# Stacking the recurrence's gate product in 64-channel blocks, and taking the next turn's first strip ahead, in a one-core fp32 two-block model kernel

## What is computed

```
proj = rmsnorm(x, ln1_g) @ w_in
b_a, c_a, x_a, x_b, g_b, gate_a_logit, gate_b_logit = split(proj)
y_a = b_a * causal_depthwise_conv(c_a * x_a, conv_a_w)          # 3 taps
u_b = causal_depthwise_conv(x_b, conv_b_w, conv_b_b)            # 4 taps and a bias
xh  = u_b as (512, 16 heads, 64)
r   = sigmoid(einsum('bshd,hde->bshe', xh, w_a) + b_a)          # 64 x 64 per head
i   = sigmoid(einsum('bshd,hde->bshe', xh, w_x) + b_x)
a   = exp(-8 * r * softplus(-lam));  b = sqrt(1 - a*a) * (i * u_b)
h_t = a_t * h_{t-1} + b_t                                       # scan over the 512 tokens
y_b = h * gelu(g_b)
```

## Time and profile before

| | |
|---|---|
| median of 3 runs | 1701.06 us |
| the profiled execution's own time | 1705.36 us |
| its span, first to last instruction | 1703.6 us |
| TensorE busy | 1671.0 us (98%) |
| GpSimd busy | 819.4 us (48%) |
| VectorE busy | 880.0 us (52%) |
| ScalarE busy | 643.8 us (38%) |

### The profile page before, as it was taken

One profiled execution on the slowest core, in us unless ns is written; L12 is line 12 of the kernel. 1 busy time (PEld: TensorE's weight loads), 2 busy tenths in 40 slices (PEclk: granted clock), 3 DMA queues, 4 the chain that ended last, 5 costly groups with the idle time before them and its releaser, 6 DMA issues.

```text
span 1703.6 us, 21182 instructions
## 1 busy us (share of the span) xinstructions
PE 1671.0 (98%) x7452; PEld 1362.8 (80%) x7452; DVE 880.0 (52%) x1165; ACT 643.8 (38%) x825; POOL 819.4 (48%) x604
## 2 busy tenths in 40 slices
PE   8999998999999999999999999999999999999997
PEld 5687777878878888888888888888888888888886
DVE  6688787555346434344557676743333432232235
ACT  6534333544323111121245757563333432222222
POOL 4446245735325444444436656554444444444443
PEclk9999999999999999999999999999999999999998
DMA  5123222333112223222233333333222332223233
GB/s 214 60 75 99 87 62 87 99 123 112 62 62 89 97 98 99 98 93 92 98 99 99 113 110 111 104 106 98 98 90 95 99 98 97 92 95 99 98 99 99
DMA packets 48783, 166.51 MB, mean 98 GB/s; under 512 B 5269, under 2 KB 7445, under 8 KB 48474
## 3 DMA queue, kind: packets, MB, share of 16 engines
q1 hardware_dynamic: 44864, 158.51, 28.2%
q10 hardware_dynamic: 3866, 7.28, 1.3%
HBM read 163.66 MB, written 2.11 MB: 97 GB/s over the span
## 4 chain that ended last, share of the span: by engine, by line
PE 38%; issue 25%; POOL 20%; DVE 2%; POOLq 0%; DMA 0%; ACT 0%; DVEq 0%; SPq 0%
POOL m_w_lo L557 19%; PE ps L637 13%; PE ps L639 13%; PE ps L638 13%; POOL m_QL L598 0%; DVE m_h L2542 0%; PE ps L832 0%; DVE m_cbuf L1986 0%; DMA m_raw<-in_strips 0%; POOLq L574 0%; DVE m_ctmp L1984 0%; POOLq L572 0%; PE ps L779 0%; DVE ps L2128 0%; DVE m_s L2119 0%
## 5 line engine op out<-in xcount | busy, mean ns | idle before, releaser
L557 POOL TENSOR_TENSOR m_w_lo<-m_raw,m_w_hi 128x512 fp32r<-128x512 f32 x582 | 786.7, 1374 | 832.3 <-ACT m_w_hi L1235 832.0
L1235 ACT ACTIVATE m_w_hi<-m_raw 128x1024 fp32r<-128x1024 f32 x291 | 307.0, 1057 | 627.9 <-DMA m_raw<-in_strips 627.8
L637 PE MATMUL ps<-m_XH,m_w_hi 128*128 128x512 f32 x1096 | 437.5, 399 | 3.6 <-POOL m_w_lo L557 3.1
L639 PE MATMUL ps<-m_XH,m_w_lo 128*128 128x512 f32 x1096 | 427.8, 390 | 0.0
L638 PE MATMUL ps<-m_XL,m_w_hi 128*128 128x512 f32 x1000 | 390.3, 390 | 0.0
L637 PEld LDWEIGHTS ps<-m_XH,m_w_hi 128*128 128x128 f32 x1096 | 206.5, 188 | 53.8 <-issue 6.6
L639 PEld LDWEIGHTS ps<-m_XH,m_w_lo 128*128 128x128 f32 x1096 | 206.2, 188 | 43.6
L638 PEld LDWEIGHTS ps<-m_XL,m_w_hi 128*128 128x128 f32 x1000 | 188.3, 188 | 41.8 <-issue 3.9
L637 PE MATMUL ps<-m_FH,m_w_hi 128*128 128x512 f32 (+1 forms) x438 | 169.3, 387 | 0.4 <-DVE m_FL L1771 0.4
L639 PE MATMUL ps<-m_FH,m_w_lo 128*128 128x512 f32 (+1 forms) x438 | 169.1, 386 | 0.0
L638 PE MATMUL ps<-m_FL,m_w_hi 128*128 128x512 f32 (+1 forms) x438 | 169.1, 386 | 0.0
(11 more groups left out here) (397 smaller groups left out, 2195.6 us busy)
## 6 DMA issues: line engine op xcount, KB each, us to landing
m_raw<-in_strips SPq DMA_DIRECT2D x294, 512.0 KB, 3.3
m_x_in<-in_x SPq DMA_DIRECT2D x4, 512.0 KB, 8.2
m_spread<-g_kept ACTq DMA_DIRECT2D x8, 256.0 KB, 3.3
m_x_res<-in_x ACTq DMA_DIRECT2D x1, 2048.0 KB, 9.2
m_memf<-in_mem SPq DMA_DIRECT2D x1, 1024.0 KB, 15.9
m_decay<-in_decay ACTq DMA_DIRECT2D x1, 1024.0 KB, 10.2
out<-m_h SPq DMA_DIRECT2D x8, 128.0 KB, 1.8
out<-m_h ACTq DMA_DIRECT2D x8, 128.0 KB, 1.8
```

The lines of the kernel that those rows point to most:

```text
L557: nc.gpsimd.tensor_tensor(w_lo[:, c], raw[:, c], f(w_hi[:, c]), ALU.subtract).then_inc(lo_ready, 1)
L637: pe.matmul(dst, hi[:, c], xh, start=first, stop=False)
L639: return pe.matmul(dst, lo[:, c], xh, start=False, stop=last)
L1235: act.activation(w_hi[:, c], raw[:, c], ACT.Copy).then_inc(hi_ready, 1)
```

## The change

- **Gates.** The convolved u of 128 channels is two blocks of 64. For each block one tile `uS[block]` holds the rounded u in one half of its partitions and the rest of u in the other half. The weights of the block stand twice, once for each half, and the columns are gate a (64) and gate x (64). One matmul of high weights with `uS` then gives high x high and high x low at once, and one of low weights follows: 2 matmuls a block, 4 a turn in place of 6. Only 256 of the strip's columns are used now, and GpSimd subtracts those alone (`gates_low`), in two pieces of 128 columns. To make the tiles, ScalarE rounds u in two activations of 64 partitions, VectorE subtracts in two operations of 64 partitions, and ScalarE applies the sigmoids in four activations of 64 partitions, which also put the gates back in order.
- **First strip ahead.** Scaling and convolving the first strip of turn t + 1 (`x_scaled`, `x_convolved`, `x_tapped`) stand within the recurrence of turn t. For turn 0 they stand ahead of the loop.
- **Order on ScalarE and VectorE.** `ahead(n + 1)` and `ahead(n + 2)` stand behind u's rounding now. The scaling of `h` stands ahead of the wait for `atap`.

```diff
+            def gates_low(slot):
+
+                for block in range(2):
+                    c = slice(slot * STRIP + block * P, slot * STRIP + (block + 1) * P)
+                    nc.gpsimd.tensor_tensor(w_lo[:, c], raw[:, c], f(w_hi[:, c]), ALU.subtract).then_inc(lo_ready, 1)
...
-                    for g in range(2):
-                        mm = three(ps[:, 5 + g, :], (S_IN + n) % RING, g, uH[:], uL[:], True, True)
+                    for block in range(2):
+                        c = slice((S_IN + n) % RING * STRIP + block * P, (S_IN + n) % RING * STRIP + (block + 1) * P)
+                        pe.matmul(ps[:, 5 + block, :], w_hi[:, c], uS[block][:], start=True, stop=False)
+                        mm = pe.matmul(ps[:, 5 + block, :], w_lo[:, c], uS[block][:], start=False, stop=True)
...
+            def x_tapped(mt):
+
                 act.wait_ge(in_free[0], mt + 1)
                 act.activation(xtap[:], pX[:, 3:T + 3], ACT.Identity, bias=col("cbb", mt), scale=col("cb3", mt)
                                ).then_inc(x_tap, 1)
+
+            def lru_turn(mt):
+
+                n = S_IN + mt * 6
+                act.wait_ge(u_full, mt + 1)
+                for block in range(2):
+                    r = slice(block * 64, (block + 1) * 64)
+                    act.activation(uS[block][r, :], t2[1][r, :], ACT.Copy).then_inc(u_high, 1)
+                ahead(n + 1)
                 ahead(n + 2)
-                act.wait_ge(u_full, mt + 1)
-                act.activation(uH[:], t2[1][:], ACT.Copy).then_inc(u_high, 1)
                 act.wait_ge(a_in, mt + 1)
...
-                act.activation(t2[6][:], ps[:, 5, :], ACT.Sigmoid, bias=col("ba", mt)).then_inc(achain, 1)
-                act.activation(t2[7][:], ps[:, 6, :], ACT.Sigmoid, bias=col("bx", mt)).then_inc(gates_free, 1)
+                for gate, name in ((6, "ba"), (7, "bx")):
+                    for block in range(2):
+                        r, q = slice(block * 64, (block + 1) * 64), slice((gate - 6) * 64, (gate - 5) * 64)
+                        act.activation(t2[gate][r, :], ps[q, 5 + block, :], ACT.Sigmoid,
...
                 if mt < KT - 1:
                     ahead(n + 6)
+                    x_tapped(mt + 1)
...
+            ahead(S_IN)
+            root(4)
+            root(5, acc)
+            x_tapped(0)
             for mt in range(KT):
                 lru_turn(mt)
...
                 ch.add(dve.tensor_tensor(t2[7][:], t2[7][:], t2[1][:], ALU.mult))
+                if mt < KT - 1:
+                    x_scaled(mt + 1)
                 dve.wait_ge(lru_e, mt + 1)
                 ch.sync()
                 dve.scalar_tensor_tensor(s0[:], a_sq[:], 1.0, t2[10][:], ALU.add, ALU.mult).then_inc(lru_q, 1)
+                if mt < KT - 1:
+                    x_convolved(mt + 1)
```

More of the change, by code:

```diff
@@ L246, in build @@
         BL = at("BL", KT * T, 144 * KB, F32R)
-        uH = at("uH", T, 160 * KB, F32R)
-        uL = at("uL", T, 162 * KB, F32R)
+        uS = [at("uS0", T, 160 * KB, F32R), at("uS1", T, 162 * KB, F32R)]
         pX = at("pX", T + 3, 164 * KB)
@@ L624, in _ @@
             product_low(1, 2)
-            lows(S_HY + 18, N_STRIPS)
+            lows(S_HY + 18, S_IN)
+            with pool.Fori(0, KT // 2) as i:
+                for u in range(12):
+                    pool.wait_ge(hi_ready, i * 12 + (S_IN + u + 1))
+                    if u % 6 < 5:
+                        low((S_IN + u) % RING)
+                    else:
+                        gates_low((S_IN + u) % RING)
+            lows(S_MG, N_STRIPS)
         @block.tensor
@@ L1149, in in_turn @@
                     pe.wait_ge(lo_ready, (i * 12 + (S_IN + n + 1)) * 2)
-                    pe.wait_ge(u_pair, mt + 1)
+                    pe.wait_ge(u_pair, mt * 2 + 2)
                     if not first:
-                        pe.wait_ge(gates_free, mt)
-                    for g in range(2):
-                        mm = three(ps[:, 5 + g, :], (S_IN + n) % RING, g, uH[:], uL[:], True, True)
+                        pe.wait_ge(gates_free, mt * 2)
+                    for block in range(2):
+                        c = slice((S_IN + n) % RING * STRIP + block * P, (S_IN + n) % RING * STRIP + (block + 1) * P)
+                        pe.matmul(ps[:, 5 + block, :], w_hi[:, c], uS[block][:], start=True, stop=False)
+                        mm = pe.matmul(ps[:, 5 + block, :], w_lo[:, c], uS[block][:], start=False, stop=True)
                     mm.then_inc(pe_done, 1)
@@ L1692, in lru_turn @@
                 act.wait_ge(pe_done, n + 6)
-                act.activation(t2[6][:], ps[:, 5, :], ACT.Sigmoid, bias=col("ba", mt)).then_inc(achain, 1)
-                act.activation(t2[7][:], ps[:, 6, :], ACT.Sigmoid, bias=col("bx", mt)).then_inc(gates_free, 1)
+                for gate, name in ((6, "ba"), (7, "bx")):
+                    for block in range(2):
+                        r, q = slice(block * 64, (block + 1) * 64), slice((gate - 6) * 64, (gate - 5) * 64)
+                        act.activation(t2[gate][r, :], ps[q, 5 + block, :], ACT.Sigmoid,
+                                       bias=const[r, COL[name] + mt:COL[name] + mt + 1]
+                                       ).then_inc(gates_free if gate == 7 else achain, 1)
                 ahead(n + 5)
-                act.wait_ge(gates_free, mt + 1)
+                act.wait_ge(gates_free, 2 * mt + 2)
                 act.activation(t2[8][:], t2[6][:], ACT.Exp, scale=col("rate", mt)).then_inc(lru_a, 1)
@@ L2393, in _, with conv_step, x_scaled, x_convolved @@
             ch.sync()
+            def conv_step(mt, dst, src, name, prev):
+                ch.sync()
+                return dve.scalar_tensor_tensor(dst[:], src, col(name, mt), prev[:], ALU.mult, ALU.add)
+            def x_scaled(mt):
+                dve.wait_ge(pe_done, S_IN + mt * 6 + 1)
+                dve.tensor_tensor(pX[:, 3:T + 3], ps[:, 0, :], rstd[:], ALU.mult).then_inc(in_free[0], 1)
+            def x_convolved(mt):
+                dve.wait_ge(in_free[0], mt + 1)
+                dve.wait_ge(x_tap, mt + 1)
+                ch.add(conv_step(mt, t2[2], pX[:, 2:T + 2], "cb2", xtap))
+                ch.add(conv_step(mt, t2[0], pX[:, 1:T + 1], "cb1", t2[2]))
+                conv_step(mt, t2[1], pX[:, 0:T], "cb0", t2[0]).then_inc(u_full, 1)
+            x_scaled(0)
+            x_convolved(0)
             for mt in range(KT):
                 n = S_IN + mt * 6
[L2398 to L2408, removed]
                 dve.wait_ge(pe_done, n + 2)
@@ L2411, in _ @@
                 dve.wait_ge(u_full, mt + 1)
-                dve.wait_ge(u_high, mt + 1)
-                dve.tensor_tensor(uL[:], t2[1][:], f(uH[:]), ALU.subtract).then_inc(u_pair, 1)
+                dve.wait_ge(u_high, 2 * mt + 2)
+                for block in range(2):
+                    r, q = slice(block * 64, (block + 1) * 64), slice((1 - block) * 64, (2 - block) * 64)
+                    dve.tensor_tensor(uS[block][q, :], t2[1][r, :], f(uS[block][r, :]), ALU.subtract
+                                      ).then_inc(u_pair, 1)
                 dve.wait_ge(pe_done, n + 3)
@@ L2419, in _ @@
                 dve.sem_inc(in_free[2], 1)
+                if mt == 0:
+                    dve.wait_ge(norm_rstd, 6)
+                ch.add(dve.scalar_tensor_tensor(tile(h, mt), tile(h, mt), col("fin_g", mt), acc[:],
+                                                ALU.mult, ALU.mult))
                 dve.wait_ge(a_tap, mt + 1)
-                ch.add(conv_step(s1, pA[:, 1:T + 1], "ca1", atap))
-                ch.add(conv_step(t2[9], pA[:, 0:T], "ca0", s1))
+                ch.add(conv_step(mt, s1, pA[:, 1:T + 1], "ca1", atap))
+                ch.add(conv_step(mt, t2[9], pA[:, 0:T], "ca0", s1))
                 dve.wait_ge(pe_done, n + 4)
@@ L2436, in _ @@
                 dve.tensor_tensor(t2[4][:], ps[:, 4, :], rstd[:], ALU.mult).then_inc(in_free[4], 1)
-                dve.wait_ge(gates_free, mt + 1)
+                dve.wait_ge(gates_free, 2 * mt + 2)
                 ch.add(dve.tensor_tensor(t2[7][:], t2[7][:], t2[1][:], ALU.mult))
+                if mt < KT - 1:
+                    x_scaled(mt + 1)
                 dve.wait_ge(lru_e, mt + 1)
@@ L2624 @@
             for b in range(2):
-                lru[b * 64:(b + 1) * 64, g * P + b * 64:g * P + (b + 1) * 64] = w[2 * m + b]
+                for side in range(2):
+                    lru[side * 64:(side + 1) * 64, b * P + g * 64:b * P + (g + 1) * 64] = w[2 * m + b]
         parts.append(np.stack([x_b[m], c_a[m], x_a[m], b_a[m], g_b[m], lru]))
```

4 lines of the change are left out of this document (removed).

## The result

The changed kernel takes 1712.88 us (median of 9 runs, 1707.75 to 1716.99) against 1701.91 us for the kernel before (9 runs, 1699.21 to 1708.96). The ratio is 1.006, with a 95% interval of 1.0047 to 1.0074. It is slower by 11.0 us by medians, where I forecast 2.3 us less. The profiled execution of the changed kernel took 1715.03 us, with a span of 1713.2 us.

A forecast was written before the change was run, and what follows sets the result against it. TensorE, 98% busy, and the ScalarE and VectorE chain were taken as nearly equal bounds (28.6 against 29.0 us a turn). 3.6 + 3.3 - 2.9 - 1.7 = 2.3 us less than 1701.06: 1698.7 us, range 1695.8 to 1701.9.

The forecast's parts named there:

- Matmuls: TensorE in the recurrence: two fewer matmuls in each of 8 turns, 3.6 us less.
- seams: Between the turns of the recurrence: TensorE's waits, eight counted, 3.3 us in all, would go.
- The chain of a turn: From the gates' end to the next first strip's low halves: 22.1 to 27.3 us, due at 27.9.
- rival D: Recurrence turns: ScalarE and VectorE work outgrows TensorE's; slower, 1706.7 us at a miss of 1 us; chance 0.10.
- h in atap's shadow: In each turn, scaling h beside atap (0.75 to 1.66 us) is hidden and delays only yA.
- Half-height work: Operations of 64 partitions in each turn: two more sigmoids at 0.59 us, subtractions at most 0.93 us each.
- Turn 0: TensorE starts the fifth strip 2.2 to 3.1 us late, taken as 2.9, its rounding now behind xtap and u.
- The clock: Behind the wait at turn 0's fifth strip: TensorE's clock falls to 1.2 GHz, costing 1.7 us.
- Other covers: Other roundings in the turns stay in time: fifth strip's low halves by 18.0 us, due at 21.6.

The follow-up runs named there:

- stacked gates alone: The kernel before with only the new gates (4 matmuls a turn, 64-partition operations), all orders as before: 1718.05 us, ratio 1.0081.
- orders alone: The changed kernel with the gates as before (6 matmuls, full height), h still scaled ahead of atap: 1702.00 us, ratio 0.9986.

## Why the prediction was wrong

- **Matmuls, 3.6 us, and seams, 3.3 us:** right in size, but the seams didn't go in the changed kernel. Two turns take 28.11 us there; with h behind yA all do, and the sum comes out: 226.5 - 3.6 - 3.3 + 2.4 (turn 0) = 222.0, as measured.
- **The chain of a turn:** this is the step that failed: "The chain is in time by 0.6 to 5.8 us; TensorE becomes the bound". Its sum began at the end of the gates, with ScalarE in time. From the sigmoids (1060.96) to GpSimd's end (1083.92 + 2.96 = 1086.88) it measures 25.9 us, within my 22.1 to 27.3. But the sigmoids began 4.3 us late, so that it ended 30.3 us behind the gates' last matmul, and was due at 27.9. Of these 2.4 us TensorE was itself 1.2 late by the seam before, and 1.2 is what the next seam costs. The loop that binds doesn't pass through TensorE; it runs from yA through AH, a rounding, a table load and the sigmoids to the next yA. I wrote that the scaling of h "delays only yA", and named that queue under rival D, without summing it. A whole turn of that loop in the new order was the sum to make.
- **h in atap's shadow, nothing:** mis-sized. It cost 1.27 us a turn (4.03 to 5.30), 0.22 of it uncovered and 1.05 by the race for the shared ports. That contention was in my rows (750 against 1659 ns), but for the chain of a turn I used it as a range; I asked who starts first only in turn 0.
- **Half-height work:** I took 0.59 us from one sigmoid to the next, as before; it is 0.71, and the half-height work lengthens the loop by 2.1 us a turn in all (stacked gates alone). With this work at full height the loss is gone as well, so it is as much a part of the cause as h's place.
- **Turn 0, 2.9 us late:** 2.89 in the changed kernel, 2.4 with h behind yA. The mechanism and size were right: h fell into GpSimd's pair as I had assumed (3.15 us with it, 2.70 without).
- **The clock, 1.7 us:** it fell behind that wait in the profiled execution, as forecast, for 3.4 us. That was partly luck: behind the same wait of 2.89 us it stayed at 1.00 in the version with h ahead of pA.
- **Other covers:** I followed the roundings of the turns, and not the one behind the last turn. The merging stage lost 6.0 us: 3.1 to the wait for it, and most of the rest to the clock behind it. No rival of mine had this.
- **Rival D** named the side of the result, and the queue that did it, but not the condition: contention was not at its worst in every step (25.9 of 27.3 us). It priced a miss of 1 us a turn at 1706.7; the seams missed by about that much from the end of turn 3 on, five of eight, and the merging stage adds its 6 us.

With the two missing terms the sum closes. The five seams cost 5.5 us (1.2 each, the first 0.8). In the recurrence -3.6 - 3.3 + 2.9 + 1.7 + 5.5 = 3.2, and 3.5 were measured; with the 6.0 of the merging stage the two stages are 9.5 us longer, of the 11.0 between the medians. Undoing h's place is worth 15 us by medians, of which the profiled executions show 8.0 in the recurrence (230.0 to 222.0) and 5.5 in the merging stage (180.0 to 174.5). Not all of that is the loop itself: 1.7 us of the 8.0, and about half of the 5.5, is time at the lower clock that only the changed kernel's execution had.

## What to carry to other kernels

When engines pass work around a loop, write down one whole turn from an operation back to itself, in the new order, and do not assume that any engine is in time; the engine that is 98% busy need not be on that loop. An operation put into another's shadow is free only if what follows it doesn't then meet an operation that it used to precede: here a shift of 0.22 us turned a won race for a shared port into a lost one, for 1.05 us more. And look one stage past the edited loop: what ends late there delays the first work of the next.

## What the runs showed of the hardware

- **Half-height activations don't overlap.** Full ones of 0.69 us start 0.59 us apart (939.75 and 940.34); four of 64 partitions take 0.68 each and 2.81 us together, 0.71 apart, and a full rounding behind them starts only after their end too (1063.80 against 1063.77). No run tells whether the height or the change of partitions between them does it.
- **Who starts first, by 0.01 or 0.2 us, decides.** The same two operations, a tap of VectorE and GpSimd's pair, take 1.82 and 2.96 us in one order and 0.75 and 3.40 in the other. This is the exclusive lock of the Trainium skill (SBUF — State Buffer, Who interferes with whom). The traces agree with it in that the one that starts second is the one that takes longer; the sum of the two also differs, 4.78 against 4.15 us.
- **The clock is not the same in each execution of one code.** In the kernel before it fell to 0.51 behind the waits until 246 and 366 us, and a third time, from 273.8 to 277.3, behind a wait of 3.54 us (until 272.82) that the prediction left out. In the version with h behind yA, whose code there is the same, it stayed up behind its waits of 3.13 us (until 246.44) and 1.80 us (until 361.25), and behind the 2.44 us in turn 0 too:

```profile
246.50:250.00 3.50, 3.50 (x16) 2.62 (x17) 3.40 (x9) 1.32 (x2) 0.00 (x0) 1.00 0.26 90
361.30:364.80 3.50, 3.50 (x15) 2.62 (x16) 0.45 (x1) 0.00 (x0) 3.50 (x3) 1.00 1.03 389
898.50:902.00 3.50, 3.44 (x15) 2.84 (x16) 3.43 (x4) 0.08 (x1) 3.50 (x5) 1.00 0.12 47
```

  Its recurrence begins 5.9 us earlier (879.83 against 885.73), with the same code ahead of it; three such stretches at 1.7 us are 5.1 (an estimate). At turn 0's fifth strip the length of the wait alone doesn't decide it either: behind 1.92 us (orders alone) it fell to 0.51 and behind 2.89 us (the changed kernel) to 0.50, while behind 2.44 us (h behind yA) and another 2.89 us (h ahead of pA) it stayed at 1.00. The clock goes with a kernel's scatter of some 8 us from lowest to highest: of the nine executions of the changed kernel the fastest (1707.75 us) had a mean clock of 0.996, the two slowest (1716.44 and 1716.99) 0.990. That is why stages are compared here, and not only totals. What decides it stays open.
